# Copying turned tiles on ScalarE, and routing three of four token tiles under the fourth norm

## What is computed

```python
x = layer_norm(alpha * x + (1.0 + gt1) * mix, ln1_w[l], ln1_b[l])     # mix = (...) @ w_o
u2 = layer_norm(x) * (1.0 + sc2) + sh2
# moe_ffn, its routing and its shared expert:
scores = jax.nn.sigmoid(ut.astype(f32) @ router_w.astype(f32))
sel = scores + router_b.astype(f32)
grp_score = jnp.sum(lax.top_k(grp, 2)[0], -1)                         # 8 groups of 8 experts
_, gidx = lax.top_k(grp_score, TOPK_GROUPS)
_, eidx = lax.top_k(jnp.where(emask, sel, -jnp.inf), TOP_K)
w_sel = w_sel / jnp.sum(w_sel, -1, keepdims=True) * ROUTED_SCALE
shared = (jax.nn.silu(ut @ sh_gate) * (ut @ sh_up)) @ sh_down
```

## Time and profile before

| | us |
|---|---|
| median of 3 runs | 1864.26 |
| lowest and highest | 1862.16, 1869.86 |
| the profiled execution, its own time | 1870.8 |
| its span | 1869.0 |
| TensorE, VectorE, ScalarE, GpSimd busy in it | 1660.1, 1361.9, 797.5, 432.4 |

### The profile page before, as it was taken

One profiled execution on the slowest core, in us unless ns is written; L12 is line 12 of the kernel. 1 busy time (PEld: TensorE's weight loads), 2 busy tenths in 40 slices (PEclk: granted clock), 3 DMA queues, 4 the chain that ended last, 5 costly groups with the idle time before them and its releaser, 6 DMA issues. The chain is left out here.

```text
span 1869.0 us, 42378 instructions
## 1 busy us (share of the span) xinstructions
PE 1660.1 (89%) x15366; PEld 1200.8 (64%) x15366; DVE 1361.9 (73%) x2538; ACT 797.5 (43%) x1321; POOL 432.4 (23%) x424
## 2 busy tenths in 40 slices
PE   3999999999378888788787789999999999999976
PEld 2787766787277677666534466767667676766632
DVE  3699998653467877775556578878888887888718
ACT  1322223442245554543300156666666566666501
POOL 2000000060456655461013011121212121121200
PEclk9899999999679999898987889999999999999988
DMA  8634854341512332232243179999999898999745
GB/s 278 199 102 147 267 181 130 118 134 64 129 38 60 78 78 56 66 64 52 104 164 146 53 269 352 377 373 350 363 358 365 342 354 337 356 345 351 286 179 238
DMA packets 260081, 387.89 MB, mean 208 GB/s; under 512 B 121986, under 2 KB 195904, under 8 KB 232815
## 3 DMA queue, kind: packets, MB, share of 16 engines
q1 hardware_dynamic: 239680, 352.18, 54.1%
q0 software_dynamic: 19904, 33.60, 4.9%
q10 hardware_dynamic: 367, 0.22, 0.1%
HBM read 366.23 MB, written 58.49 MB: 227 GB/s over the span
## 5 line engine op out<-in xcount | busy, mean ns | idle before, releaser
L2463 DVE TENSOR_TENSOR moe_w_lo<-pre,moe_w_hi 128x1024 fp32r<-128x1024 f32 x272 | 314.9, 1220 | 2.2
L2389 ACT ACTIVATE moe_w_hi<-pre 128x1024 fp32r<-128x1024 f32 x272 | 265.1, 1048 | 17.1 <-SPq L2227 9.6
L2342 PE MATMUL moe_pY<-moe_wd,moe_hT 128*128 128x512 f32 x544 | 244.8, 593 | 0.5 <-ACT moe_hT L2404 0.5
L2332 PE MATMUL moe_pH<-moe_w_hi,moe_x_hi 128*128 128x512 f32 x544 | 219.2, 403 | 10.9 <-issue 8.1
L572 PE MATMUL proj_bank<-u_hi,w_hi 128*128 128x512 f32 x536 | 213.2, 398 | 5.9 <-PEq L74 4.4
L2332 PE MATMUL moe_pH<-moe_w_lo,moe_x_hi 128*128 128x512 f32 x544 | 214.2, 394 | 0.0
L2332 PE MATMUL moe_pH<-moe_w_hi,moe_x_lo 128*128 128x512 f32 x544 | 214.2, 394 | 0.0
L572 PE MATMUL proj_bank<-u_hi,w_lo 128*128 128x512 f32 x536 | 209.5, 391 | 0.0
L572 PE MATMUL proj_bank<-u_lo,w_hi 128*128 128x512 f32 x536 | 209.1, 390 | 0.0
L2261 POOL DMA_INDIRECT moe_xg<-scratch_u2d,moe_idx x70 | 71.0, 1015 | 479.2 <-ACT moe_y L2410 300.9
L798 DVE SCALAR_TENSOR_TENSOR proj_hc<-proj_hp,cwT,proj_hc 128x512 f32<-128x512 f32 x240 | 162.1, 743 | 0.0
(11 more groups left out here) (417 smaller groups left out, 3019.5 us busy)
## 6 DMA issues: line engine op xcount, KB each, us to landing
pre<-in_exp_gate SPq DMA_DIRECT2D x68, 1024.0 KB, 7.3
pre<-in_exp_up SPq DMA_DIRECT2D x68, 1024.0 KB, 10.7
moe_wd<-in_exp_down SPq DMA_DIRECT2D x68, 1024.0 KB, 11.6
w<-in_w_in SPq DMA_DIRECT2D x59, 512.0 KB, 4.0
pre<-in_ada_w SPq DMA_DIRECT2D x10, 2048.0 KB, 9.2
last_yb<-scratch_ybuf SPq DMA_DIRECT2D x3, 2560.0 KB, 25.8
scratch_rkv<-proj_st SPq DMA_DIRECT2D x24, 256.0 KB, 2.0
last_yb<-scratch_ybuf SPq DMA_DIRECT2D x3, 1536.0 KB, 29.0
```

Source lines behind the costliest of these rows:

```text
L2332: ins = nc.tensor.matmul(pH[:], a[:, k], w[p][:, k].rearrange("p w f -> p (w f)"), start=(k == 0 and n == 0), stop=(k == KC - 1 and n == 2))
L2342: ins = nc.tensor.matmul(pY[h][:], hT[:, f], wd[q][:, f, h * 512:(h + 1) * 512], start=(f == 0), stop=(f == 1))
L2389: nc.scalar.activation(w_hi[p][:, ks].rearrange("p k w f -> p w k f"), raw[p][:, :, ks], ACT.Copy) \
L2463: nc.vector.tensor_tensor(w_lo[p][:, ks].rearrange("p k w f -> p w k f"), raw[p][:, :, ks], w_hi[p][:, ks].rearrange("p k w f -> p w k f") ...
```

## The change

Five things are altered, all in `mix_and_route`; nothing is computed otherwise.

- The copies from PSUM to `u2T` go from VectorE (its loop of eight copies is removed) to ScalarE, as `turned(t)`.
- Tiles 0 to 2 are turned one after the other into banks 0 to 5, and tile 3 into banks 0 and 1; the logits go to bank 6 (tiles 0 to 2) and bank 7 (tile 3). The waits on `tp_read` between halves are gone; `route(t)` waits for the copies of its own tile.
- TensorE no longer turns all four tiles before it routes: it turns and routes tiles 0 to 2, multiplies the first shared product of f = 0 over their 384 tokens, and only then waits for tile 3. The last 128 tokens of both products come behind the logits of tile 3. Banks 2 to 5 hold the shared products.
- ScalarE takes the sigmoid of tiles 0 to 2 when those three have logits, so VectorE may select for them before tile 3 is routed.
- `shared_up(1, 0)` is cut in two halves around the small product that counts blocks, and `shared_up(1, 1)` goes behind the last three small products.

```diff
-            for t in range(TT):
-                pe.wait_ge(u2_ready, t + 1)
-                for h in range(2):
-                    n = 2 * t + h
-                    if n >= 2:
-                        pe.wait_ge(tp_read, n - 1)
...
-            pe.wait_ge(tp_read, 2 * TT)
...
+            for t in range(TT - 1):
+                if t == 0:
+                    pe.wait_ge(mix_read, 2 * TT)
+                turn(t)
+            pe.wait_ge(rt_in, 32)
+            for t in range(TT - 1):
+                route(t)
             pe.wait_ge(sh_in, 32)
+            shared_up(0, 0, most, (0, KC))
+            turn(TT - 1)
+            shared_up(0, 1, most, (0, KC))
+            route(TT - 1)
             for w in range(2):
-                shared_up(0, w)
+                shared_up(0, w, rest_, (0, KC)).then_inc(h_done, 1)
...
-            shared_up(1, 0)
+            shared_up(1, 0, slice(0, T), (0, 4))
             pe.wait_ge(nb_ready, 1)
             nc.tensor.matmul(bank[0][0:E, 0:1], upto[0:E, 0:E], nb[:], start=True, stop=True).then_inc(ci_done, 1)
-            shared_up(1, 1)
+            shared_up(1, 0, slice(0, T), (4, KC)).then_inc(h_done, 1)
...
+            shared_up(1, 1, slice(0, T), (0, KC)).then_inc(h_done, 1)
...
+            def turned(t):
+                for h in range(2):
+                    act.wait_ge(tp_done, 2 * t + h + 1)
+                    nc.scalar.activation(u2T[:, 4 * h:4 * h + 4, t * P:(t + 1) * P],
+                                         bank[(2 * t + h) % 6][:].rearrange("p (k t) -> p k t", k=4), ACT.Copy).then_inc(tp_read, 1)
...
+            for n in range(2 * TT - 2):
+                deviation(n)
+            for t in range(2):
+                turned(t)
+            deviation(2 * TT - 2)
+            turned(2)
+            deviation(2 * TT - 1)
+            for t in range(TT - 1):
+                scores(t)
+            turned(TT - 1)
+            scores(TT - 1)
...
-            for n in range(2 * TT):
-                t, h = n // 2, n % 2
-                v.wait_ge(tp_done, n + 1)
-                nc.vector.tensor_copy(u2T[:, 4 * h:4 * h + 4, t * P:(t + 1) * P],
-                                      bank[n % 2][:].rearrange("p (k t) -> p k t", k=4)).then_inc(tp_read, 1)
```

More of the change, by code:

```diff
@@ L2008, in _, with route @@
                                                   g["ident"][:])
                     ins.then_inc(tp_done, 1)
-            pe.wait_ge(tp_read, 2 * TT)
-            pe.wait_ge(rt_in, 32)
-            for t in range(TT):
+            def route(t):
+                pe.wait_ge(tp_read, 2 * t + 2)
                 for k in range(KC):
-                    ins = nc.tensor.matmul(bank[2][:, t * E:(t + 1) * E], u2T[:, k, t * P:(t + 1) * P], rw[:, k],
+                    ins = nc.tensor.matmul(bank[6 + t // (TT - 1)][:, t * E:(t + 1) * E], u2T[:, k, t * P:(t + 1) * P], rw[:, k],
@@ L2015, in _, with shared_up @@
                                            start=(k == 0), stop=(k == KC - 1))
                 ins.then_inc(logit, 1)
-            pe.wait_ge(sh_in, 32)
[L2020 to L2024, removed]
+            def shared_up(f, w, ts, ks):
+                for k in range(*ks):
+                    ins = nc.tensor.matmul(bank[2 + 2 * f + w][:, ts], shw[:, k, w, f * P:(f + 1) * P], u2T[:, k, ts],
+                                           start=(k == 0), stop=(k == KC - 1))
+                return ins
@@ L2026, in _ @@
+            most, rest_ = slice(0, (TT - 1) * P), slice((TT - 1) * P, T)
+            for t in range(TT - 1):
[5 more added lines that the diff above has]
+                route(t)
+            pe.wait_ge(sh_in, 32)
+            shared_up(0, 0, most, (0, KC))
+            turn(TT - 1)
+            shared_up(0, 1, most, (0, KC))
+            route(TT - 1)
             for w in range(2):
-                shared_up(0, w)
+                shared_up(0, w, rest_, (0, KC)).then_inc(h_done, 1)
@@ L2030, in _ @@
             for t in range(TT):
-                ins = nc.tensor.matmul(bank[2][0:E, 0:1], A[:, t], ones[:, 0:1], start=(t == 0), stop=(t == TT - 1))
+                ins = nc.tensor.matmul(bank[6][0:E, 0:1], A[:, t], ones[:, 0:1], start=(t == 0), stop=(t == TT - 1))
             ins.then_inc(cnt_done, 1)
             for t in range(TT):
-                o = bank[3][:, t * E:(t + 1) * E]
+                o = bank[7][:, t * E:(t + 1) * E]
                 for i in range(t):
@@ L2045, in _, with deviation, scores @@
             nc.tensor.matmul(bank[1][:, P:P + 1], nbr[:], ones[0:E, 0:1], start=True, stop=True).then_inc(eb_done, 1)
+            shared_up(1, 1, slice(0, T), (0, KC)).then_inc(h_done, 1)
         @block.scalar
         def _(act):
-            for n in range(2 * TT):
+            def deviation(n):
                 act.wait_ge(var1, n + 1)
                 nc.scalar.activation(rstd[:, n:n + 1], mv[:, 1:2], ACT.Sqrt, bias=g["eps"][:, 0:1]).then_inc(std1, 1)
-            for t in range(TT):
-                act.wait_ge(logit, TT)
-                nc.scalar.activation(sc[:, t], bank[2][:, t * E:(t + 1) * E], ACT.Sigmoid).then_inc(score, 1)
+            def turned(t):
[3 more added lines that the diff above has]
+                                         bank[(2 * t + h) % 6][:].rearrange("p (k t) -> p k t", k=4), ACT.Copy).then_inc(tp_read, 1)
+            def scores(t):
+                act.wait_ge(logit, TT - 1 if t < TT - 1 else TT)
+                nc.scalar.activation(sc[:, t], bank[6 + t // (TT - 1)][:, t * E:(t + 1) * E], ACT.Sigmoid).then_inc(score, 1)
+            for n in range(2 * TT - 2):
[9 more added lines that the diff above has]
+            scores(TT - 1)
             for f in range(2):
                 act.wait_ge(h_done, 2 * f + 1)
-                nc.scalar.activation(hs[:, f], bank[4 + 2 * f][:], ACT.Silu).then_inc(sh_silu, 1)
+                nc.scalar.activation(hs[:, f], bank[2 + 2 * f][:], ACT.Silu).then_inc(sh_silu, 1)
         @block.vector
@@ L2131, in _ @@
             for j in range(3):
[L2132 removed]
+                ch.mark(nc.vector.tensor_scalar(cnt[:, j:j + 1], bank[6][0:E, 0:1], float(P * (j + 1)), None, ALU.is_gt))
             ch.wait()
```

10 lines of the change are left out of this document (5 added, 5 removed).

## The result

The changed kernel took 1853.66 us in the median of 8 runs (1851.09 to 1861.1), the kernel before 1864.33 in the median of 8 (1861.94 to 1871.9): ratio 0.9939, 95% interval 0.9920 to 0.9958, 11.4 us less (7.8 to 14.9). The forecast was 13.3 us less and 1851.0, the range 1845 to 1857.5.

The account below looks back on a forecast made before the run. TensorE and VectorE stood partly unused between 1004 and 1031, then TensorE alone bounded. A gross 15.0 us less 1.7 for the clock gave 13.3 us less, 1851.0 from the median 1864.3; range 1845 to 1857.5.

Parts of the forecast that it names:

- What bounds: Output projection to block table: TensorE and VectorE partly unused from 1004 to 1031; TensorE alone bounds after the last `A`.
- ScalarE's copies ahead of the seventh root: Turning tiles 0 to 2: four copies end at 1004.2, the root started at 1004.69; 0.4 us left, costed at nothing.
- Routing at full clock: Three tiles' 48 router records on TensorE: 5.0 us at full clock, 8.9 at 186 ns each; either early enough.
- The selection beside GpSimd: VectorE's first selection during GpSimd's tile 3 operations: its two-operand adds stand, the second until about 1016.5.
- rival (B): VectorE's small operations don't stand beside GpSimd, no TensorE pause, clock stays up: 17.6 us saved, 1846.7; chance 0.23.
- the 0.15: GpSimd's last transformation of tile 3, beside VectorE's selection, ends at 1016.5 instead of 1016.35.
- The clock behind the wait: After TensorE's 2.6 us idle for the last `A`, a clock fall costs 0 to 3.5 us; taken as 1.7.
- the gross 15.0: End of stage, before the clock term: VectorE's last shared product starts at 1048.85 instead of 1063.82, 15.0 us.
- The cut of (1,0): Shared product halved after the last `A`: gives VectorE's chain cover, ready 1039.5 against 1040.9 when TensorE wants it.
- (C): Clock stays low longer, through routing and 384-column products: saving 9 us, 1855.3; chance 0.16.
- (D): Clock never comes back in the stage, as short products and pauses alternate: 20 us late, 1885; chance 0.03.
- (E): Something else holds the barrier, a store of tile 3 or an expert's load: 1864; chance 0.05.

Follow-up runs that it names:

- late scores: The changed kernel, but ScalarE takes the sigmoid of tiles 0 to 2 only when tile 3 has its logits too; ratio 1.0017 to the kernel before.
- tile 3 on VectorE with the end undone: The changed kernel with tile 3 scaled and shifted on VectorE and f = 1's shared products in the old order; ratio 0.9935 to the kernel before.
- copies only: The kernel before, with only the eight copies moved to ScalarE, all behind its eighth square root; ratio 1.0016 to the kernel before.
- copies on VectorE: The changed kernel, but VectorE makes all eight copies, behind its fourth norm and ahead of the selections; ratio 1.0043 to the kernel before.

## Why the prediction was right

**What bounds.** Right. The hole under the fourth norm and the half-clock routing were what was to be had, and TensorE bounds again at the end (VectorE waited 9.42 us for it, 6.38 before). One remark on it was wrong: that nobody can have tile 3 ready earlier. VectorE itself had it ready 12.1 us from the first transpose, GpSimd at 15.9.

**ScalarE's copies ahead of the seventh root.** Right that they cost nothing: four in 2.07 us, ending 1.5 us before the root is wanted. I had counted on 0.4; the root came later, since VectorE's residual add (L2112) stood for GpSimd's tile 2 and took 2.67 us instead of 1.95.

**Routing at full clock.** 48 records in 5.3 us (forecast 5.0 to 8.9).

**The selection beside GpSimd.** The choice that decided between the forecast and rival (B) was right: the adds over 64 and over 8 elements stood as the one over 1024 had. The first stood until 1011.42, just after GpSimd's first operation ended at 1011.33; the second, of 8 elements, stood until 1013.78, the second one having ended at 1013.75. The maxima between them took 0.64 as always. The Trainium skill (SBUF — State Buffer, "Who interferes with whom") says that a VectorE instruction with two SBUF inputs contends with a GpSimd instruction that reads SBUF, and names no size. The traces agree, 1.89 and 1.65 us against 0.23 and 0.17 alone. GpSimd's operations took 2.35 and 2.34 and were not held up, so the 0.15 that I added for that was not there. What I had not counted was that the residual add would stand 0.7 us longer than in before, with all behind it.

**The clock behind the wait: the term that failed.** I took 1.7 us for a fall behind the pause for `A`. In four executions of this kernel there was none. I had put the fall in the wrong pause: TensorE idled 2.6 us ahead of tile 3, the clock fell 1 us later, and the product (0,1) took 7.0 instead of 5.3 us. That cut the pause for `A` to 0.84 us instead of 2.6, and cost nothing by itself: `A` less what the add stood is 28.45 with this fall and without it. So the stage gained 14.6, close to the gross 15.0, and not 13.3; with the add standing alike in both it would be 15.3. For a pause like the forecast's 2.6 the bounds of 0 and 3.5 held, in the kernels in which it stayed: 0 behind 2.17 us, 3.4 behind 2.54. They were not bounds of the whole term: 4.4 behind 3.25 and 5.0 behind 12. The forecast had 1.4 us for the table's products at half clock, half of their 2.84; they took 5.2 there (late scores, and tile 3 on VectorE with the end undone), 2.4 more.

**The time.** The forecast's 13.3 lies in the measured interval (7.8 to 14.9), and that is in part luck: it was 1.3 us short of the profiled stage's gain, and 1.9 over that of the times, 11.4. The first comes mainly from the clock term, taken at 1.7 and measured at 0, less the 0.7 that the add stood longer. The second is open, as said above. If before's profiled execution had a long stage, the step was to take that execution as typical: the forecast corrected its time to the median, and not the length of its stage.

**The cut of (1,0).** The forecast credited it with cover. It wasn't needed: without it the way from `A` to the end was 0.8 us shorter.

**Rivals.** (C) and (D) fell, the clock was at 1.00 for all but 3.3 us; (E) fell, the barrier followed VectorE's last instruction by 1.6 us as before.

## What to carry to other kernels

Look for the engine that is free while the chain's last piece is in work, and move to it what the next step needs: neither the engine (copies only) nor the order (copies on VectorE) gained by itself, and without the early scores the gain was nil. Before an instruction is moved beside GpSimd, see if it reads two operands from SBUF. Measure from an event at the stage's start: the stage repeated within 0.3 us where whole executions scattered by 9. But before a difference of a us or so is put down to an edit, see if instructions that both kernels share took the same time: here one add in front of everything moved the stage by up to 1.44 us.

## What the runs showed of the hardware

- Shortening TensorE's work ahead of a wait can cost what it brings. Behind waits of 2.54 and 3.25 us, where the changed kernel had 0.84, the clock was at 0.50 and the end came 3.4 and 4.4 us later; a fall earlier, beside other slack, was free.
- The clock does not follow the length of a pause alone: 2.17 us of it had no fall behind it, 1.76 us (behind ten us of steady products) had one.
- An add over 8 elements, 0.17 us alone, took 1.65 us beside a GpSimd operation with SBUF operands; eight MAX over 8 elements each, 0.64 us together, took no longer there.
- Which of the two stands depends on which was there first: a GpSimd add over 1024 elements took 3.22 us instead of 2.35 where VectorE's add was ahead of it, and VectorE's 2.67 instead of 1.23 where GpSimd's was.
- The block table's small products took 5.2 us at 0.50 and 2.8 at 1.00.
